# Half swaps of the rotary embedding by on-chip transfers instead of matmuls, and two reorderings on the vector engine, in a two-block transformer kernel

## The reference

```python
def rope(x, pos_f):
    half = x.shape[-1] // 2
    ...
    return jnp.concatenate([x1 * cos - x2 * sin, x1 * sin + x2 * cos], axis=-1)

def mla_group(c_q, c_kv, k_pe_raw, pos_f, q_norm, w_uq, kv_norm, w_ukv):
    q = (rms_norm(c_q, q_norm) @ w_uq).reshape(B, S, H, QK_NOPE_DIM + QK_ROPE_DIM)   # 8 heads, 64 + 32
    q_pe = rope(q[..., QK_NOPE_DIM:], pos_f)
    kv = (rms_norm(c_kv, kv_norm) @ w_ukv).reshape(B, S, H, QK_NOPE_DIM + V_HEAD_DIM)
    k_pe = rope(k_pe_raw[:, :, None, :], pos_f)[:, :, 0]                             # one key of 32 shared by all heads
    s = q_nope @ k_nope + q_pe @ k_pe;  p = softmax(s * MLA_SCALE);  return p @ v

def swiglu_2(x, w_gate, w_up, w_down):
    return (jax.nn.silu(x @ w_gate) * (x @ w_up)) @ w_down                           # 1024 -> 2816 -> 1024
```

## Time and profile before

| quantity | value |
|---|---|
| median of 3 runs | 1930.81 us (1929.57 to 1934.14) |
| profiled execution: its time / its span | 1930.77 us / 1929.0 us |
| PE busy | 1895.4 us, 98% of the span |
| DVE / ACT / POOL busy | 74% / 53% / 45% |
| DMA queues | q1 32.4% of 16 engines' span |

### The profile page before, as it was taken

The page is one execution under the profiler, slowest core; times in us unless marked ns, Lnnn a source line. Parts: engine busy times, 40 slices in busy tenths (PEclk is TensorE's granted clock), DMA queues, the critical chain, the costliest instruction groups (busy, mean ns, idle before and its releaser), DMA issues. The chain is left out here.

```text
span 1929.0 us, 38346 instructions
## 1 busy us (share of the span) xinstructions
PE 1895.4 (98%) x13929; PEld 1747.0 (91%) x13929; DVE 1423.9 (74%) x1940; ACT 1025.4 (53%) x1704; POOL 868.4 (45%) x521
## 2 busy tenths in 40 slices
PE   8999999999999999999999999999999999999998
PEld 8999999997779899989989999897875778999898
DVE  5987797785456877787787777967766549777887
ACT  5566554525324566664466666545346435666543
POOL 3455453643325454552555555254541034555623
PEclk9999999999999999999999999999999999999999
DMA  6233333322412233333423333344521022333332
GB/s 180 66 100 107 93 103 102 97 59 66 114 52 66 85 112 99 108 110 88 121 66 110 103 104 110 89 109 123 125 56 44 2 87 77 110 108 106 101 88 88
DMA packets 345997, 180.09 MB, mean 93 GB/s; under 512 B 19211, under 2 KB 340486, under 8 KB 345886
## 3 DMA queue, kind: packets, MB, share of 16 engines
q1 hardware_dynamic: 344176, 177.56, 32.4%
q10 hardware_dynamic: 1710, 1.01, 0.2%
HBM read 174.35 MB, written 2.10 MB: 91 GB/s over the span
## 5 line engine op out<-in xcount | busy, mean ns | idle before, releaser
L3522 PE MATMUL ps<-xop,whi 128*128 128x256 f32 (+1 forms) x4032 | 721.9, 281 | 5.3 <-ACT wa L877 2.9
L3522 PEld LDWEIGHTS ps<-xop,whi 128*128 128x128 f32 x4032 | 620.1, 188 | 7.7 <-ACT wa L877 3.5
L3522 PE MATMUL ps<-xop,wlo 128*128 128x256 f32 (+1 forms) x2016 | 568.0, 282 | 0.0
L548 POOL TENSOR_TENSOR wlo<-raw,whi 128x1024 fp32r<-128x1024 f32 x94 | 234.8, 2506 | 362.7 <-ACT whi L719 347.4
L3522 PEld LDWEIGHTS ps<-xop,wlo 128*128 128x128 f32 x2016 | 380.0, 188 | 0.0
L609 POOL TENSOR_TENSOR wlo<-raw,whi 128x512 fp32r<-128x512 f32 x212 | 279.1, 1327 | 223.6 <-ACT whi L859 222.6
L3460 PE MATMUL ps<-xop,whi 128*128 128x256 f32 (+1 forms) x896 | 214.8, 284 | 5.0 <-issue 4.0
L3188 PE MATMUL ps<-xhi,whi 128*128 128x512 f32 (+2 forms) x624 | 208.5, 363 | 2.0 <-DVE xlo L1904 1.9
L3188 PE MATMUL ps<-xlo,whi 128*128 128x512 f32 (+2 forms) x624 | 204.0, 356 | 0.0
L3188 PE MATMUL ps<-xhi,wlo 128*128 128x512 f32 (+2 forms) x624 | 203.9, 356 | 0.0
L3460 PE MATMUL ps<-hid_r,whi 128*128 128x256 f32 (+1 forms) x768 | 190.3, 282 | 0.5 <-POOL wlo L656 0.3
(11 more groups left out here) (467 smaller groups left out, 3958.0 us busy)
## 6 DMA issues: line engine op xcount, KB each, us to landing
raw<-in_ffn_w_in SPq DMA_DIRECT2D x88, 512.0 KB, 3.8
raw<-in_ffn_w_gate SPq DMA_DIRECT2D x44, 512.0 KB, 3.8
raw<-in_ffn_w_up SPq DMA_DIRECT2D x44, 512.0 KB, 3.9
raw<-in_ffn_w_out SPq DMA_DIRECT2D x32, 512.0 KB, 4.4
raw<-in_ffn_w_down SPq DMA_DIRECT2D x32, 512.0 KB, 4.4
raw<-in_a_w_in SPq DMA_DIRECT2D x24, 512.0 KB, 4.1
raw<-in_w_in SPq DMA_DIRECT2D x19, 512.0 KB, 4.0
raw<-in_ffn_w_out SPq DMA_DIRECT2D x16, 384.0 KB, 3.5
```

What stands on the lines that cost most here:

```text
L548: pool.tensor_tensor(wlo[:, u % SLOTS, :], raw[:, u % SLOTS, :], whi[:, u % SLOTS, :].bitcast(F32), ALU.subtract).then_inc(lo_done, 1)
L3522: ins = pe.matmul(to, w[l][:, k * P:(k + 1) * P], x[r][:, k * h:(k + 1) * h], start=start and k == 0 and q == 0, stop=k == 3 and q == 2, s ...
```

## The change

Three parts.

1. The half swaps of the shared key and of both groups of attention queries are made by transfers issued by SP: eight for each tile, of 16 partitions each, 16 partitions being half of a 32-wide head. The key's go into `sq`, after the load of unit 11; the queries' into the attention's buffer `PT`, in `load_units` at units 28 and 29 (`SWAP_AT`), each ahead of that unit's load. The three PE instructions go away. The sign now comes from a column of constants, as the scale of ACT's sine. PE's wait for `kept_dve` 1, which stood ahead of `swap(1)`, stays where it is.
2. In `dve_down`, at d = 0, the low part of S4 is made ahead of the low part of A22 instead of after three more instructions; `LO_DVE` follows.
3. In the first step of `dve_ffn`'s body, `s4` of the next step runs ahead of `gate`.

```diff
@@ SP
     def swap_halves(sp, r):
-        x, half = (m2["rq"] if r < 5 else m2["rk"])[:, (r - 1) % 4, :], RET_DIM // 2
         sp.wait_ge(a2["raw_ready"], r + 4)
-        sp.wait_ge(a2["swap_used"], r)
-        for o in range(0, P, RET_DIM):
+        if r == 0:
+            sp.wait_ge(a2["cstat"], 2)
+            move_halves(sp, sq[:, 0:SEQ], m2["kpe"][:, :], ROPE_DIM, a2["swapped"])
+        else:
+            sp.wait_ge(a2["swap_used"], r)
+            move_halves(sp, sq[:, 0:SEQ], (m2["rq"] if r < 5 else m2["rk"])[:, (r - 1) % 4, :], RET_DIM, a2["swapped"])
+    SWAP_AT = 28
+    def move_halves(sp, to, x, dim, sem):
+        half = dim // 2
+        for o in range(0, P, dim):
             for a, b in ((o, o + half), (o + half, o)):
-                sp.dma_start(sq[a:a + half, 0:SEQ], x[b:b + half, :]).then_inc(a2["swapped"], 16)
+                sp.dma_start(to[a:a + half, :], x[b:b + half, :]).then_inc(sem, 16)
+    def swap_queries(sp, g):
+        sp.wait_ge(a3["kept_dve" if g else "kept_act"], 1)
+        if g == 1:
+            sp.wait_ge(a3["swap_used"], 1)
+        move_halves(sp, m3["PT"][:, 0, 0:SEQ], m3["qp"][:, g, :], ROPE_DIM, a3["swapped"])
     def load_units(sp, u0, units):
...
-            if u0 == U_M2 and 1 <= j - 12 < 9:
+            if u0 == U_M2 and 0 <= j - 12 < 9:
                 swap_halves(sp, j - 12)
+            if u0 == U_M2 and j in (SWAP_AT, SWAP_AT + 1):
+                swap_queries(sp, j - SWAP_AT)
             slot_read(sp, u)
@@ ACT, second mixer
-                               scale=m2["invf"][:, 4:5] if j == 1 else 1.0).then_inc(s["trig"], 1)
+                               scale=m2["invf"][:, 5 - j:6 - j]).then_inc(s["trig"], 1)
@@ tables of the downward half
-    LO_DVE += [("T3", 0), ("T3", 1), ("S3", 0), ("B22", 0), ("A22", 0), ("B22", 1), ("S4", 0), ("T4", 0), ("A11", 1), ("T4", 1)]
+    LO_DVE += [("T3", 0), ("T3", 1), ("S3", 0), ("B22", 0), ("S4", 0), ("A22", 0), ("B22", 1), ("T4", 0), ("A11", 1), ("T4", 1)]
@@ dve_ffn, body(st)
+            if first:
+                s4(nxt)
             gate(st)
-            if not last:
+            if not first and not last:
                 s4(nxt)
@@ dve_down
         post(0, "u2", "M6", 0, 1, a)
+        lo(0, "S4")
         lo(0, "A22")
         post(0, "k5", "M5", 1, 1, c)
         x_lo("B22", 1)
-        lo(0, "S4")
@@ dve_mla, rope(g)
-            v.wait_ge(s["swapped"], g + 1)
-            v.tensor_tensor(tmp, m3["sinm"][:, :], ps[:, 2 + 3 * g, :], ALU.mult).then_inc(s["swap_used"], 1)
+            v.wait_ge(s["swapped"], 128 * (g + 1))
+            v.tensor_tensor(tmp, m3["sinm"][:, :], m3["PT"][:, 0, 0:SEQ], ALU.mult).then_inc(s["swap_used"], 1)
@@ pe_mix2 and pe_mla
-            if e == 4:
-                swap_k_pe()
...
         pe.wait_ge(s["kept_act"], 1)
-        swap(0)
         pe_query(pe, 2)
...
         pe.wait_ge(s["kept_dve"], 1)
-        swap(1)
         pe.wait_ge(s["kept_act"], 3)
         pe_query(pe, 5)
```

More of the change, by code:

```diff
@@ L88 @@
 for _name, _cols in [("ident", P), ("ones", P), ("tri", P), ("pairs", HEADS // 2 * P),
-                     ("permpe", P), ("block", P), ("invf", 5), ("tabs", 4 * P)]:
+                     ("permpe", P), ("block", P), ("invf", 6), ("tabs", 4 * P)]:
     CONST[_name] = slice(_n, _n + _cols)
@@ L121, in constants @@
     c[:, CONST["invf"].start + 3] = p
+    c[:, CONST["invf"].start + 5] = np.where(p % ROPE_DIM < ROPE_DIM // 2, -1.0, 1.0)
     c[:, CONST["invf"].start + 4] = np.where(p % RET_DIM < RET_DIM // 2, -1.0, 1.0)
@@ L197, in program @@
               ("permpe", [P, P], F32)]
-    m2, m3 = region_parts(shared, [[("cosr", [P, SEQ], F32), ("sinr", [P, SEQ], F32), ("invf", [P, 5], F32), ("lg", [P, 2 * HEADS], F32), ("lgt", [P, 2 * HEADS], F32),
+    m2, m3 = region_parts(shared, [[("cosr", [P, SEQ], F32), ("sinr", [P, SEQ], F32), ("invf", [P, 6], F32), ("lg", [P, 2 * HEADS], F32), ("lgt", [P, 2 * HEADS], F32),
                           ("rq", [P, 4, SEQ], F32), ("rk", [P, 4, SEQ], F32), ("rv", [P, CH, RET], F32),
@@ L2861, in rope @@
                 v.wait_ge(s["trig"], 2 * r + 2)
-            if r == 0:
-                v.wait_ge(s["swapped"], 1)
-            else:
-                v.wait_ge(s["swapped"], 1 + 64 * r)
-            turned = ps[rows, 6, :] if r == 0 else sq[:, 0:SEQ]
+            v.wait_ge(s["swapped"], 128 + 64 * r)
+            turned = sq[:, 0:SEQ]
             v.tensor_tensor(tmp, m2[si][rows, :], turned, ALU.mult).then_inc(s["swap_used"], 1)
@@ L3814, in pe_mix2 @@
         s, u0 = a2, U_M2
-        def swap_k_pe():
-            pe.wait_ge(s["raw_ready"], 4)
-            pe.wait_ge(s["const"], 64)
-            pe.matmul(ps[:, 6, :], m2["permpe"][:, :], m2["kpe"][:, :], start=True, stop=True).then_inc(s["swapped"], 1)
         def sum_mixed(k):
@@ L3958, in pe_mla @@
         s, u0 = a3, U_M2 + 20
-        def swap(g):
-            pe.matmul(ps[:, 2 + 3 * g, :], m3["permpe"][:, :], m3["qp"][:, g, :], start=True, stop=True) \
-              .then_inc(s["swapped"], 1)
         pe.wait_ge(s["kept_act"], 1)
-        swap(0)
         pe_query(pe, 2)
```

## The result

The changed kernel takes 1953.43 us (median of 5 runs, 1951.99 to 1954.6) against 1931.0 us of the kernel before, run beside it. The ratio is 1.0110, with a 95% interval of 1.0099 to 1.0121: 1.1% slower. The forecast was slower by 1.0%, at 1950.6. The profiled execution took 1953.58 us, with a span of 1951.8 us, 22.8 longer than before.

What follows compares the result with a forecast made beforehand. PE, busy 98% of the span, was taken to bound the kernel. Queries +17.1, clock +4.0, key -0.8, S4 -3.0 and gate +2.5 sum to +19.8 us on 1930.77: 1950.6 us, range 1941 to 1957 (about 0.85).

Steps and rivals of the forecast that it cites:

- The queries' first swap: Attention's beginning: eight transfers issued behind the fifth `w_o` load land at 1458.3, so PE stands 5.6 us before query tile 5.
- The rival of short issues: Attention's query transfers: half the partitions cost half the issue, 4.2 us less, 1946.4 us; chance 0.22 shared with no clock fall.
- The queries' second swap: Attention's beginning: transfers behind the sixth `w_o` load land at 1476.9, so the first scores start 17.1 us late in all.
- only the first swap stalls: Rival at the attention's beginning: the second swap is released early, first scores 3.9 us late, total 1935.4 us; chance 0.04.
- TensorE's clock: After the attention's two stalls PE runs at half speed for a while: +4.0 us, bounds 0 to 9.5.
- the rival without a fall: After the attention's stalls the clock stays up or slow work is off the chain: 1946.6 us; chance 0.22 shared with short issues.
- The shared key: Its swap leaves PE and the transfers land in time for DVE: -0.8 us, with 0 as the other end.
- The cover of 1.6 us: Shared key: transfers land at 1342.6, ahead of DVE's first instruction on it at 1344.21; if not, PE reads results much later.
- S4: Feed-forwards' downward halves: its earlier low part shortens three PE waits by 1.0 us each, -3.0 us, bounds 1.8 and 4.0.
- The gate: Feed-forwards' first steps: the gate behind the fourth sum delays SiLU and PE's wait on ACT's copy: +2.5 us, bounds 0 to 3.5.
- The sum: Whole kernel: 17.1 + 4.0 - 0.8 - 3.0 + 2.5 = +19.8 us on 1930.77, giving 1950.6 us.

## Why the prediction was right, point by point

**The queries' first swap.** Predicted: eight issues of 0.60 us behind the fifth load, 2.0 to land, PE stands 5.6 us. Measured: 5.01 us for eight, DVE at work 6.46 us after the first issue (predicted 4.2 + 2.0 = 6.2), PE stands 5.80. The doubtful term was the issue of 16 partitions, and it costs what 32 do. The rival of short issues is refuted.

**The queries' second swap.** Predicted: the sixth load 4.89 us after `values(0)`, DVE 6.6 us later, PE stands 11.5 us, key copies 3.2 us after the rope's start. Measured: `values(0)` started at 1470.45 and the load at 1475.32, 4.87 later; DVE started 6.81 after that; PE stood 11.58 and then 0.97 for the copies. The waits of 18.35 us, less the two products of 0.84, are 16.7 against the predicted 17.1. The run with the first set early and the one with both sets behind the fifth load show the parts: 15.4 us for the second place alone, 8.0 for the first, and 2.3 when both are early. So it is the place in the queue, more than the transfers. The rival "only the first swap stalls" priced the query part at 5.9 us; the run that comes nearest to it, with both sets behind the fifth load, measured 8.0 in the stretch.

**TensorE's clock.** Predicted +4.0, between 0 and 9.5. Measured: the stretch is 22.2 us longer and the waits explain 16.7, so 5.5 us are the half speed; half of the 5.4 and 5.7 us of slow work comes to the same. That the clock would fall was right, and the rival without a fall is refuted. The 4.0 was no more than a point a little under the middle of a wide range, so its nearness to 5.5 is partly luck. The picture taken from the earlier trace rows was of work following one long idle time; what the trace adds is that the clock is still full in the first 4 us of each wait. By the Trainium skill (TensorE: Matmul & The Clock Gate, What's actually happening) the low level is the default and activity releases it; the waits fit. The low stretches near 366 and 961 stand behind no wait of that kind: PE is marked busy in them, and just ahead of them it ran matmuls of one column.

**The shared key.** Predicted -0.8, measured -0.84 in the changed kernel. The cover of 1.6 us was not there: the eight issues took 5.02 us, so the last began at about 1344.1, and DVE was released by it 3.6 us later, not 2.0. DVE waited after all.

```profile
sq<-kpe SPq DMA_DIRECT2D x8, 32.0 KB, 2.6
...
1339.69 5.02 SPq L495 DMA_DIRECT2D sq<-kpe  x8
...
1347.74 0.69 DVE L2886 TENSOR_TENSOR wa<-sinm,sq 128x512 f32<-128x512 f32 x1 [0.27 <-DMA sq<-kpe]
```

As the prediction said of that case, PE did not notice.

**S4.** Predicted -3.0, as three times 1.0 out of waits of 1.3, because T4's last low part stands 0.8 us behind, so that PE can be at most 1.4 us earlier there. Measured alone: -3.5 by the ratio (-1.7 to -5.2). The step is right in kind and size. Laid beside before's row by row, the changed kernel's PE is 1.5 us earlier at M3 of the third feed-forward and 1.3 at the second half of T4, where it waits the 0.26 us shown above; by the start of mixer 2 it has lost a further 0.7, in pieces of 0.1 to 0.4. The even price per feed-forward was not quite right. In the third it is 0.6. In the first, S4 alone against the second profile of before (same pace, both with a low stretch at 366) is 1.1: 493.96 and 495.05 us from PE's wait at 79 to the one on DVE at 573 to 574. In the fourth it is 0.7 to 1.4. A later wait on DVE there, 0.86 us in the first profile, is gone with the new order, but with the old order it stood in only five of nine profiles (0.29 to 0.91). The four with the queries placed elsewhere had none, and a mean of 273.7 against the new order's 273.0. So the 2.7 us that the changed kernel gains there on before's profile are in part luck of that pair.

**The gate: the term with the widest spread.** Predicted +2.5, as 0.75 for each of three feed-forwards and 0.3 for the first, with 3.5 as the end. The delay itself came out as worked: `s4` did not start earlier, the SiLU came 1.08 us later, PE 1.05, and in the first feed-forward PE's wait grew from 1.44 to 1.95. Little was absorbed, 0.18 us of the next wait and 0.2 in mixer 2. What was missing is the clock: in both profiles with this order a wait of 2.2 us was followed by 3.4 us at half speed in two places; the waits of 1.2 us there never were. Over the stretches of the table the gate alone costs 1.0 + 1.8 + 1.1 - 0.2 + 1.0 = 4.7 us, and 0.5 more in the first feed-forward. Its median says less: +2.7 by the ratio (1.0 to 4.4), which is the predicted size; that the low clock did not come in every execution of that kernel can explain a part of the difference. Taken out of the changed kernel it is 4.8 by the medians and 6.6 by the ratios (3.3 to 9.9). So the prediction's 2.5 agrees with the run of the order alone and is 2 to 4 us short in the changed kernel; the two intervals overlap, so how much of that is noise stays open.

**The sum.** The prediction's 19.8 us stand against 22.8 in the profile and 21.2 (19.1 to 23.4) by the ratio. The terms, against the profiles: queries with clock 21.1 and 22.2 (18.7 by the ratio of that run); key -0.8 and -0.8; S4 -3.0 and -2.4 to -3.1; gate +2.5 and 4.7 to 5.2 (2.7 by its ratio). The shortfall of the total is in the clock's two terms, behind the queries' stalls and behind the gate.

## What to carry to other kernels

A transfer put into an in-order queue costs what stands ahead of it: find the wait of the load in front, and check that it does not depend on the very work that the transfer is to release. Work moved off a saturated engine by small transfers paid 0.5 to 0.6 us of issue each here; eight of them are dearer than the product of 0.84 us that they replace, unless all of it is hidden. And a new wait of the matmul engine can cost more than its length: in the changed kernel's profile those of 2.2, 5.8 and 11.6 us were followed by 3.4, 5.4 and 5.7 us of work at half speed. Last, two profiles of one unchanged kernel differ by 2.2 us here, so a part worth 1 us has to be read in its own stretch, beside several profiles.

## What the runs showed of the hardware that was not expected

- Granted clock and waits: a stretch at the low level of 3.4 us began 0.3 to 1.4 us after the end of PE's waits of 2.2 us in both profiles that have them, but not in every execution (one of the eleven with the gate alone has a mean clock of 0.999); around the wait of 5.8 us the low stretch was 6.8 long and around that of 11.6 us 13.7, both from about 4.5 us into the wait. The waits of 1.96 us in the first feed-forward and of 1.56 in the fourth were followed by none.
- In twelve of the thirteen profiles, the unchanged kernel's second among them, one to three further stretches of 3.4 us at half clock stood near 365, 375 or 960 (once at 396), with PE busy. Each of these 24 stretches had a run of 10 to 18 single-column matmuls in the 4 us ahead of it. The same runs stand in the first profile of before, with no low stretch behind them. The low stretches cost 0.6 us net at 366 and nothing at 960, so they explain little of the spread of the kernel before, 1929.88 to 1933.61; the two paces of the first feed-forward, 1.3 us apart at full clock, explain more.
- A transfer of 16 partitions (32 KB) costs SP 0.62 us to issue, about as much as one of 32 partitions (64 KB) with 0.60; POOL takes 0.50.
